# GpSimd instead of VectorE divides the attention probabilities by their sums

## The chip, the cores and the metric

The kernel runs on one core of a Trainium2 chip. The metric is the device time of one execution in microseconds (us); the core has a TensorE (PE), a VectorE (DVE), a ScalarE (ACT), a GpSimd (POOL) and a SyncE (SP), each with its own instruction queue, and they meet through semaphores that the kernel sets and waits for by hand.

## The reference, cut to what matters

Two layers of a trunk over 512 latent and 256 context tokens of width 1024, in float32. Both layers hold an attention with 8 heads; the rest (gated MLP, convolution module, ConvFFN, norms) stays as it is. In the first layer queries of latent tokens see all 768 keys, queries of context tokens the 256 context keys; in the second only the latent queries are needed. The part that matters is the softmax of `block_attention`:

```python
s = jnp.einsum('bqgrd,bkgd->bgrqk', q_blk, k, preferred_element_type=jnp.float32) * scale
p = jax.nn.softmax(s, axis=-1).astype(v.dtype)
return jnp.einsum('bgrqk,bkgd->bqgrd', p, v)
```

The division in it is done on the unnormalised probabilities exp(s - max): every row of 768 (or 256) values is multiplied by the reciprocal of its sum.

## The kernel before, in words

The whole network is one program. Each engine runs one long list of steps; the order of the steps is written out by hand, and counters (semaphores) say what may start. Both attentions use the same four functions: `attn_pe`, `attn_act`, `attn_dve` and, in the second alone, `attn_pool`. The first attention (semaphore family "eva") has 40 units, numbered from 0: units 0 to 31 are a head and a tile of 128 latent queries against 768 keys, units 32 to 39 a head and two tiles of context queries against 256 keys. The second (family "od") has 32 units, a head and a tile of 128 queries against 768 keys each.

A unit u goes this way. PE computes the scores (three matmuls for each bank in the first attention, five in the second, since float32 operands are split into a high and a low part). DVE takes the row maximum (L1624) and scales it (L1626). ACT takes the exponential and, in the same pass, the row sums `rsum` (L1594, with an accumulator read). DVE inverts the sums (L1632), drains its pipeline, and multiplies the probabilities in place by the inverse, one operand row at a time (`normalise`, L1635); its semaphore "p" lets PE transpose the probabilities (L1565). ACT copies the transposed ones to `PTe`/`PTo` (L1610), PE multiplies them with V (L1580), and DVE copies the result out (L1654).

The order on the queues: in its iteration u PE does transposes of u, scores of u+2, product with V of u, then what is put beside the unit. ACT does the exponential of u+1, the copy of the transposed u, the query copy of u+3 (L1503). DVE does `normalise(u+1)`, `maxima(u+2)`, in the first attention the low part of the query u+3, the copy out of u, then the work beside the unit. In the second attention that work is a part of the depthwise convolution of width 31: `conv_steps` (L2589, one tap on 128x512 values), three taps beside each of the units 2 to 13 and two beside the others, until all 124 are done. Beside the units stand also the pieces: projections of the second half of the keys and values on PE (units 0 to 5 for values, 7, 9, ..., 21 for keys, in turn 512 and 256 columns wide), with the subtraction of DVE for a key piece one unit later (L2697). POOL forms the low part of the queries in the second attention (`q_low` in `attn_pool`, L1662) and adds up channels near the end (L1886, L1889, L1896); in the first attention it gates the MLP half (L1864) and copies V (L1866), and is then idle until the output norm.

`Pe` has three buffers, `Pod` two, the sums `rsum` two.

Of the kernel before, what the change touches and what calls it, by code (L numbers as in the profile page):

```python
# [18 lines left out]
P = 128  # L19
F32 = mybir.dt.float32  # L20
F32R = mybir.dt.float32r
ALU = mybir.AluOpType
# [42 lines left out]
def build(nc, x, ctx, cvec, wpack, modw, modu, modb, normg, ffcw, rope_ev, rope_od, qkg, aln, wsT, bs,  # L65
          odcw, odcln, gcq, gckv, out):
    es = ExitStack()
    with es:
# [54 lines left out]
        rsum = const("rsum", [P, 2, 2])  # L123
# [485 lines left out]
        TURNED = (0, 2, 1, 3)  # L609
# [95 lines left out]
        def turned_place(g, t):  # L705

            return half_tokens(g, *((0, 0), (1, 1), (0, 1), (1, 0))[t])

        def turned_sum(dve, g, t):

            if t == 0:
                dve.wait_ge(S("pre3", "hi"), since("pre3", "hi") + KD * (g + 1))
                dve.wait_ge(S("pre3", "lo_even"), since("pre3", "lo_even") + KD // 2 * (g + 1))
            if t == 1:
                dve.wait_ge(S("pre3", "lo_odd"), since("pre3", "lo_odd") + KD // 2 * (g + 1))
            dve.drain()
            b11, b12, b21, b22 = (half_tokens(g, k, h) for k in range(2) for h in range(2))
            x, y = ((b12, b11), (b22, b11), (b22, b12), (b21, b22))[t]
            nc.vector.tensor_tensor(turned_place(g, t), x, y, ALU.subtract).then_inc(S("sv", f"tsum{g}"), 1)

        def turned_hi(act, g, t):

            act.wait_ge(S("sv", f"tsum{g}"), TURNED.index(t) + 1)
            if t == 3:
                act.wait_ge(w_used, F11 + 1)
            nc.scalar.activation(TH["ff1"][t][:, :, g, :], turned_place(g, t), ACT.Copy).then_inc(S("sv", "thi"), 1)
# [778 lines left out]
        def q_low(dve, u):  # L1505
# [3 lines left out]
            nc.vector.tensor_tensor(qTl[u % 2][:, 0:n], PS[:, 6, 0:n], qTh[u % 2][:, 0:n].bitcast(F32),  # L1509
                                    ALU.subtract).then_inc(S("eva", "qTl"), 1)  # L1510

        def attn_pe(pe, st, odd, U, lead=lambda: None, extra=lambda u: None):
            PT, Pb = (PTo, Pod) if odd else (PTe, Pe)

# [70 lines left out]
        def attn_act(act, st, odd, U, scale, extra=lambda u: None, values=lambda tiles: None):  # L1585
            PT, Pb = (PTo, Pod) if odd else (PTe, Pe)

            def exps(u):
                w, n = U[u][2], U[u][3] * P
                if u >= len(Pb):  # L1590
                    act.wait_ge(S(st, "ptr"), u - len(Pb) + 1)
                act.wait_ge(S(st, "max"), u + 1)
                for i in range(w):
                    last = nc.scalar.activation(Pb[u % len(Pb)][:, i * n:(i + 1) * n],  # L1594
                                                ps2(2 * (u % 2), w * n)[:, i * n:(i + 1) * n], ACT.Exp,
                                                bias=rmax[:, u % 2, i:i + 1], scale=scale,
                                                accum_out=rsum[:, u % 2, i:i + 1])
                last.then_inc(S(st, "exp"), 1)
# [16 lines left out]
        def attn_dve(dve, st, odd, U, scale, cat, extra):  # L1615
# [12 lines left out]
            def normalise(u):  # L1628
# [7 lines left out]
                                                   ALU.mult)  # L1636
                last.then_inc(S(st, "p"), 1)

            maxima(0)
            maxima(1)  # L1640
            if not odd:
                q_low(dve, 2)
            normalise(0)
            for u, (h, t, w, nk, k0) in enumerate(U):
                if u + 1 < len(U):
                    normalise(u + 1)
                if u + 2 < len(U):
                    maxima(u + 2)
                if u + 3 < len(U) and not odd:
# [7 lines left out]
        def attn_pool(pool, st, U, extra):  # L1657
# [5 lines left out]
                                        ALU.subtract).then_inc(S(st, "qTl"), 1)  # L1663
            for u in range(2):
                q_low(u)
            for u in range(len(U)):
                if u + 2 < len(U):
                    q_low(u + 2)
                extra(u)

        def rotate(dve, x0, x1, cs, sn, tA, tB):
# [154 lines left out]
        def _(pool):  # L1826
# [34 lines left out]
            for c in range(NT):  # L1861
# [2 lines left out]
                nc.gpsimd.tensor_tensor(cc, cc, Zv[:, c, :].rearrange("p (g q) -> p g q", q=P), ALU.mult)\  # L1864
                    .then_inc(S("gate", "gated"), 1)
            nc.gpsimd.tensor_copy(Vev[:, :, :], V32[:, :, :]).then_inc(S("gate", "vev"), 1)  # L1866
            out_then_norm_pool(pool, "evo", "pre1", NT)
            out_then_norm_pool(pool, "ffo0", "pre2", NT)
            power(pool, "odq", rstd[:, 0:LT])
# [982 lines left out]
```

## Time and the profile before

| | us |
|---|---|
| median of 3 runs (lowest to highest) | 1696.81 (1695.31 to 1699.03) |
| the profiled execution, its own time | 1694.81 |
| its span, first to last instruction | 1693.0 |
| PE, DVE, ACT, POOL busy in it | 1644.3, 1342.7, 824.9, 195.6 |
| mean granted TensorE clock | 0.996 |

The busy times come from the page of the profile. Durations of one instruction come from that one execution, whose own time is 1.8 us more than its span and 2.0 us less than the median. Line numbers (L...) are those of the kernel before. Where a row gives a time in brackets, that is how long the engine sat idle before the instruction, and who ended the wait.

### The profile page before, as it was taken

The numbers are of one execution on the slowest core, as the hardware profiler recorded it, in microseconds if no ns is written. First come the engines' busy times: TensorE is split into PE (matmuls) and PEld (weight loads), VectorE is DVE, ScalarE is ACT, GpSimd is POOL, SyncE is SP. The second block draws the span as 40 slices with busy tenths as digits, with TensorE's granted clock in tenths as the row PEclk, the third lists the DMA queues.
The fourth block names the chain that finished last, engine by engine and source line by source line (L and its number), as shares of the span: only waits on it lengthen the run. The fifth ranks groups of instructions, "written<-read, shape, count | busy, mean of one in ns | idle before, by whom it ended". The sixth has DMA issues, their size and how long they took to land.

```text
span 1693.0 us, 25933 instructions
## 1 busy us (share of the span) xinstructions
PE 1644.3 (97%) x9738; PEld 1478.7 (87%) x9738; DVE 1342.7 (79%) x2261; ACT 824.9 (49%) x1501; POOL 195.6 (12%) x201
## 2 busy tenths in 40 slices
PE   6999999999999999999999999999999999999998
PEld 4788899888999999998887888879888899999876
DVE  5676777767888999996888788978776799998554
ACT  4343256634435555554243534454455466666442
POOL 1078510000300000000000300011210200000000
PEclk9999999999999999999999999999999999999999
DMA  9633210051322444447563322200102223322331
GB/s 353 203 142 113 29 23 1 1 211 63 125 113 101 160 170 167 173 165 305 180 216 123 140 78 96 79 1 2 51 26 91 72 75 117 109 100 101 137 111 64
DMA packets 46059, 194.10 MB, mean 115 GB/s; under 512 B 13040, under 2 KB 13552, under 8 KB 31216
## 3 DMA queue, kind: packets, MB, share of 16 engines
q1 hardware_dynamic: 37248, 187.46, 31.1%
q10 hardware_dynamic: 8688, 4.99, 1.0%
q8 instruction: 78, 1.28, 0.3%
q14 instruction: 45, 0.37, 0.1%
HBM read 180.48 MB, written 11.96 MB: 114 GB/s over the span
## 4 chain that ended last, share of the span: by engine, by line
PE 44%; DVE 5%; ACT 2%; DVEq 1%; issue 1%; DMA 0%; ACTq 0%; POOL 0%
PE PS L1162 6%; PE PS L1168 6%; PE PS L1165 6%; PE PS L820 4%; PE PS L822 4%; PE PS L821 4%; PE PS L1580 2%; PE PS L326 2%; PE PS L334 2%; PE PS L330 2%; PE PS L1565 1%; DVE w_lo L315 1%; PE PS L362 1%; PE PS L358 1%; PE PS L361 1%
## 5 line engine op out<-in xcount | busy, mean ns | idle before, releaser
L1162 PE MATMUL PS<-w_hi,a_ring 128*128 128x512 f32 x670 | 262.8, 392 | 5.2 <-DVE A_ff_lo L1242 1.7
L1165 PE MATMUL PS<-w_lo,a_ring 128*128 128x512 f32 x670 | 260.8, 389 | 0.0
L315 DVE TENSOR_TENSOR w_lo<-w_raw,w_hi 128x2048 fp32r<-128x2048 f32 x62 | 143.9, 2321 | 105.8 <-ACT w_hi L309 100.6
L309 ACT ACTIVATE w_hi<-w_raw 128x2048 fp32r<-128x2048 f32 x62 | 118.6, 1914 | 163.1 <-PE PS L1162 104.0
L820 PE MATMUL PS<-TH_ff,FH_ff 128*128 128x256 f32 (+1 forms) x608 | 187.4, 308 | 2.8 <-ACT pu_ff L836 2.8
L822 PE MATMUL PS<-TH_ff,FL_ff 128*128 128x256 f32 (+1 forms) x608 | 187.3, 308 | 0.0
L821 PE MATMUL PS<-TL_ff,FH_ff 128*128 128x256 f32 (+1 forms) x608 | 187.2, 308 | 0.0
L1162 PEld LDWEIGHTS PS<-w_hi,a_ring 128*128 128x128 f32 x670 | 125.8, 188 | 34.9 <-DVE w_lo L315 2.6
L1165 PEld LDWEIGHTS PS<-w_lo,a_ring 128*128 128x128 f32 x670 | 125.8, 188 | 25.4
L820 PE MATMUL PS<-HT,FH_ff 128*128 128x256 f32 (+1 forms) x456 | 140.3, 308 | 0.0
L821 PE MATMUL PS<-HT,FH_ff 128*128 128x256 f32 (+1 forms) x456 | 140.3, 308 | 0.0
L822 PE MATMUL PS<-HT,FL_ff 128*128 128x256 f32 (+1 forms) x456 | 140.3, 308 | 0.0
L1391 POOL TENSOR_TENSOR rstd<-rstd,halfneg 128x1 f32<-128x1 f32 x20 | 11.0, 550 | 1094.7 <-DVE rstd L1337 1094.7
L1168 PE MATMUL PS<-w_hi,a_ring 128*128 128x512 f32 x334 | 130.0, 389 | 0.0
L820 PEld LDWEIGHTS PS<-TH_ff,FH_ff 128*128 128x128 f32 x608 | 115.9, 191 | 3.1 <-issue 3.0
L822 PEld LDWEIGHTS PS<-TH_ff,FL_ff 128*128 128x128 f32 x608 | 115.9, 191 | 0.0
L821 PEld LDWEIGHTS PS<-TL_ff,FH_ff 128*128 128x128 f32 x608 | 115.9, 191 | 0.0
L689 ACT ACTIVATE FH_ff<-Sw_ff 128x512 fp32r<-128x512 f32 x152 | 94.8, 626 | 32.2 <-PE PS L822 26.8
L698 DVE TENSOR_TENSOR FL_ff<-Sw_ff,FH_ff 128x512 fp32r<-128x512 f32 x152 | 103.9, 685 | 3.5 <-ACT FH_ff L689 1.6
L358 PE MATMUL PS<-w_hi,HT 128*128 128x512 f32 (+1 forms) x272 | 103.1, 379 | 0.4 <-DVE HT L2457 0.4
L326 PE MATMUL PS<-HT,w_hi 128*128 128x256 f32 (+1 forms) x352 | 103.3, 323 | 0.0
L361 PE MATMUL PS<-w_lo,HT 128*128 128x512 f32 (+1 forms) x272 | 102.1, 375 | 0.0
(369 smaller groups left out, 4196.0 us busy)
## 6 DMA issues: line engine op xcount, KB each, us to landing
w_raw<-wpack SPq DMA_DIRECT2D x102, 1024.0 KB, 4.9
m_raw<-modu SPq DMA_DIRECT2D x80, 512.0 KB, 5.8
mod_raw<-modw SPq DMA_DIRECT2D x8, 1024.0 KB, 11.6
a_kept<-yb SPq DMA_DIRECT2D x17, 384.0 KB, 2.3
c_rows<-c_scratch SPq DMA_DIRECT2D x8, 512.0 KB, 5.1
x_kept<-X SPq DMA_DIRECT2D x1, 3072.0 KB, 9.6
A_ff<-a_kept SPq DMA_DIRECT2D x2, 1536.0 KB, 8.4
X<-x_kept SPq DMA_DIRECT2D x1, 3072.0 KB, 10.1
```

What stands on the lines that cost most here:

```text
L309: nc.scalar.activation(w_hi[r][:, :], w_raw[r][:, :], ACT.Copy).then_inc(wh_ready, 1)
L315: nc.vector.tensor_tensor(w_lo[r][:, :], w_raw[r][:, :], w_hi[r][:, :].bitcast(F32), ALU.subtract).then_inc(wl_ready, 1)
L326: mm = nc.tensor.matmul(o, wh, xh, start=start, stop=False)
L358: mm = nc.tensor.matmul(o, xh, w_hi[r][:, wc], start=k == 0, stop=False)
L361: nc.tensor.matmul(o, xh, w_lo[r][:, wc], start=False, stop=False)
L698: nc.vector.tensor_tensor(FL[st][i][:, :, :], form_source(st, s, i), FH[st][i][:, :, :].bitcast(F32), ALU.subtract)\
L820: nc.tensor.matmul(o, wh, xh, start=begins, stop=False, skip_group_check=onto)
L821: nc.tensor.matmul(o, wh, xl, start=False, stop=False, skip_group_check=onto)
L822: last = nc.tensor.matmul(o, wl, xh, start=False, stop=ends, skip_group_check=onto)
L1162: mm = nc.tensor.matmul(o, ah, w_hi[n % 2][:, wc], start=k == 0, stop=False)
L1165: mm = nc.tensor.matmul(o, ah, w_lo[n % 2][:, wc], start=False, stop=False)
L1168: return nc.tensor.matmul(o, al, w_hi[n % 2][:, wc], start=False, stop=k == kt - 1)
```

## The change

DVE keeps the inversion of the sums, in a new function `invert` with a semaphore "rcp" of its own, shared by both attentions. The multiplication goes to POOL, in a new function `normalise_pool`: in the first attention for units 8 to 39 (units 0 to 7 stay with `normalise` on DVE, since `BY_VECTOR["eva"]` is 8), in the second for all 32. In the first attention POOL runs through them behind the copy of V; in the second unit u+1 is put behind the query part of u+2 in each iteration. ACT gets one more wait ahead of the exponential of u, for "p" of u-2, because its row sums go into the same buffer. Two semaphores of the second ConvFFN, `tsum0` and `tsum1`, become one, `tsum`, with its counts adapted; nothing is reordered there.

```diff
-            nc.vector.tensor_tensor(turned_place(g, t), x, y, ALU.subtract).then_inc(S("sv", f"tsum{g}"), 1)
+            nc.vector.tensor_tensor(turned_place(g, t), x, y, ALU.subtract).then_inc(S("sv", "tsum"), 1)
...
-            act.wait_ge(S("sv", f"tsum{g}"), TURNED.index(t) + 1)
+            act.wait_ge(S("sv", "tsum"), 2 * TURNED.index(t) + g + 1)
...
+        BY_VECTOR = {"eva": 8, "od": 0}
+
+        def rcp_count(st, u):
+
+            return u + 1 - BY_VECTOR[st] + (len(units(False)) - BY_VECTOR["eva"] if st == "od" else 0)
+
+        def normalise_pool(pool, st, U, u):
+
+            Pb = Pod if st == "od" else Pe
+            w, n = U[u][2], U[u][3] * P
+            pool.wait_ge(S("att", "rcp"), rcp_count(st, u))
+            if u:
+                pool.wait_ge(S(st, "p"), u)
+            for i in range(w):
+                pr = Pb[u % len(Pb)][:, i * n:(i + 1) * n]
+                last = nc.gpsimd.tensor_scalar(pr, pr, rsum[:, u % 2, i:i + 1], None, ALU.mult)
+            last.then_inc(S(st, "p"), 1)
...
                 act.wait_ge(S(st, "max"), u + 1)
+                if u >= 2:
+                    act.wait_ge(S(st, "p"), u - 1)
...
+            def invert(u):
+                dve.wait_ge(S(st, "exp"), u + 1)
+                sm = rsum[:, u % 2, 0:U[u][2]]
+                nc.vector.reciprocal(sm, sm).then_inc(S("att", "rcp"), 1)
...
-            normalise(0)
+            if BY_VECTOR[st]:
+                normalise(0)
+            else:
+                invert(0)
             for u, (h, t, w, nk, k0) in enumerate(U):
-                if u + 1 < len(U):
+                if u + 1 < BY_VECTOR[st]:
                     normalise(u + 1)
+                elif u + 1 < len(U):
+                    invert(u + 1)
...
             for u in range(2):
                 q_low(u)
+            normalise_pool(pool, st, U, 0)
             for u in range(len(U)):
                 if u + 2 < len(U):
                     q_low(u + 2)
+                if u + 1 < len(U):
+                    normalise_pool(pool, st, U, u + 1)
                 extra(u)
...
             nc.gpsimd.tensor_copy(Vev[:, :, :], V32[:, :, :]).then_inc(S("gate", "vev"), 1)
+            for u in range(BY_VECTOR["eva"], len(units(False))):
+                normalise_pool(pool, "eva", units(False), u)
             out_then_norm_pool(pool, "evo", "pre1", NT)
```

## Rows read from the trace of the kernel before

**Rows 1.** The page: busy time by engine, and the chain by engine.

```profile
PE 1644.3 (97%) x9738; PEld 1478.7 (87%) x9738; DVE 1342.7 (79%) x2261; ACT 824.9 (49%) x1501; POOL 195.6 (12%) x201
...
PE 44%; DVE 5%; ACT 2%; DVEq 1%; issue 1%; DMA 0%; ACTq 0%; POOL 0%
```

**Rows 2.** Busy time by stretch: start:end, length, PE, PEld, DVE, ACT, POOL, granted clock, DMA.

```profile
240.00:340.00 100.00, 97.02 (x722) 89.22 (x721) 73.90 (x197) 64.15 (x142) 0.00 (x0) 1.00 0.00 1
...
1162.00:1192.00 30.00, 29.54 (x211) 26.86 (x210) 28.09 (x57) 14.17 (x31) 4.42 (x6) 1.00 0.00 1
```

**Rows 3.** The transposes, second attention: all, then starts in the timeline (start, duration).

```profile
L1565 PE MATMUL PS<-ident,Pod x192: 269/272/328, 1117.0 to 1258.4; 128*128 128x128 f32 x192
...
1171.15 0.82 PE L1565 MATMUL PS<-ident,Pod 128*128 128x128 f32 x6
...
1176.79 0.27 PE L1565 MATMUL PS<-ident,Pod 128*128 128x128 f32 x1
...
1202.99 0.82 PE L1565 MATMUL PS<-ident,Pod 128*128 128x128 f32 x6
1206.73 0.82 PE L1565 MATMUL PS<-ident,Pod 128*128 128x128 f32 x6
1211.86 0.82 PE L1565 MATMUL PS<-ident,Pod 128*128 128x128 f32 x6
```

**Rows 4.** DVE's timeline in the second attention, one iteration.

```profile
1165.92 0.15 DVE L1632 RECIPROCAL rsum<-rsum 128x1 f32<-128x1 f32 x1
1166.15 0.62 DVE L1635 TENSOR_SCALAR Pod<-Pod,rsum 128x768 f32<-128x768 f32 x1
1166.69 0.95 DVE L1624 TENSOR_REDUCE rmax<-PS 128x1 f32<-128x768 f32 x1
...
1168.16 2.08 DVE L2589 SCALAR_TENSOR_TENSOR cat_od<-G,ccw,cat_od 128x512 f32<-128x512 f32 x3
1170.16 0.16 DVE L1632 RECIPROCAL rsum<-rsum 128x1 f32<-128x1 f32 x1
```

**Rows 5.** The timeline in the first attention, from a maximum to its transposes.

```profile
274.54 0.96 DVE L1624 TENSOR_REDUCE rmax<-PS 128x1 f32<-128x768 f32 x1
275.82 0.90 ACT L1594 ACTIVATE Pe<-PS,rmax 128x768 f32<-128x768 f32 x1 [0.90 <-DVE rmax L1626]
275.83 0.82 PE L1565 MATMUL PS<-ident,Pe 128*128 128x128 f32 x6
...
276.85 0.16 DVE L1632 RECIPROCAL rsum<-rsum 128x1 f32<-128x1 f32 x1 [0.53 <-ACT Pe L1594]
277.09 0.62 DVE L1635 TENSOR_SCALAR Pe<-Pe,rsum 128x768 f32<-128x768 f32 x1
...
279.02 0.27 PE L1565 MATMUL PS<-ident,Pe 128*128 128x128 f32 x1
...
336.10 1.13 PE L1580 MATMUL PS<-PTe,Vev 128*128 128x256 f32 x4 [1.57 <-ACT PTe L1610]
```

**Rows 6.** POOL's groups: operation, names, shapes, count; busy, mean ns; idle before.

```profile
L1873 POOL COPY QRD<-QR 128x1024 f32<-128x1024 f32 x4 | 4.2, 1042 | 27.1 <-DVEq L2652 27.1
...
L1866 POOL COPY Vev<-V 128x1536 f32<-128x1536 f32 x1 | 1.5, 1457 | 0.0
```

**Rows 7.** The timeline of POOL and DVE where both read SBUF.

```profile
1152.02 0.46 POOL L1662 TENSOR_TENSOR qNl<-QTn,qNh 128x128 fp32r<-128x128 f32 x1 [4.68 <-ACT qNh L1503]
...
1209.14 1.26 POOL L1886 TENSOR_TENSOR mu<-cat_od 128x512 f32<-128x512 f32 x1 [3.56 <-DVEq L2702]
...
1209.39 1.43 DVE L1635 TENSOR_SCALAR Pod<-Pod,rsum 128x768 f32<-128x768 f32 x1
```

**Rows 8.** The timeline at the last unit of the second attention.

```profile
1257.16 0.62 DVE L1635 TENSOR_SCALAR Pod<-Pod,rsum 128x768 f32<-128x768 f32 x1
...
1257.84 0.87 PE L1565 MATMUL PS<-ident,Pod 128*128 128x128 f32 x6 [0.21 <-DVE Pod L1635]
```

**Rows 9.** The timeline at the start of the second attention: a wait without a releasing engine.

```profile
1123.67 0.96 DVE L1624 TENSOR_REDUCE rmax<-PS 128x1 f32<-128x768 f32 x1 [5.08 <-remote]
```

## The prediction

> **What bounds the kernel now.** The page first: PE is busy 97% of the span and holds by far the largest share of the chain that ended last, DVE 5% of it [rows 1]. So a lighter DVE is worth only what DVE still holds in the two stages that change. The view by stretches says how much that can be: in 100 us of the first attention PE is busy 97.02, with DVE at 73.90; in the second attention there is a stretch of 30 us where DVE is busy 28.09 [rows 2]. That stretch, near 1162 to 1192, is the only one where DVE is close to full.
>
> Next the starts of PE's transposes, one set for each unit, since they show PE's own period. In the second attention an undisturbed unit without a piece takes 3.74 us (1202.99 to 1206.73) and one with a 512-wide piece 5.13 (1206.73 to 1211.86); the piece of 256 columns gives about 4.46 by the same reading. Unit 11 takes 5.64 where 5.13 would do (1171.15 to 1176.79) [rows 3]. Added up over all units, 31 periods from 1117.0 [rows 3] to 1257.84 [rows 8] (6 of 5.13 with pieces of the values, 4 of 5.13 and 4 of 4.46 with pieces of the keys, 16 plain ones of 3.75 and unit 30 of 2.0, and two sums over channels of 0.86), the matmuls alone would fill some 133 of 141 us. The 8 us between are: 2.3 at unit 1, 1.6 over units 10 to 15, 1.4 at units 21 and 22 (PE waits for its own last piece and for the subtraction behind it), 1.0 at units 25 and 27, 1.7 at unit 30 (no scores are left to fill the wait for the copy). In the first attention the period is 3.19 (275.83 to 279.02) [rows 5], and so for all latent units from 9 to 31 within 0.04; DVE and ACT wait there for PE and for one another, and PE is never out of work.
>
> **What the change removes.** 72 multiplications on DVE: 24 of 128x768 in the first attention, 16 of 128x256 there, 32 of 128x768 in the second. One of 768 takes 0.62, and from the inversion to the maximum behind it passes 0.77 (1165.92 to 1166.69), of which the inversion and its hand-over need about 0.15 [rows 4]. So DVE gets back 0.62 for each unit of 768. Where is that on the path? In the full stretch an iteration of DVE takes 4.24 with three taps (1165.92 to 1170.16) [rows 4], up to 4.64 with the subtraction of a key piece in it, against PE's mean of (3.74 + 5.13 + 3.74 + 4.46)/4 = 4.27. With 0.62 gone it is 3.6 to 4.0: PE sets the pace again, and the 1.6 us of units 10 to 15 come back. At unit 27 the exponential waits for DVE behind a large weight subtraction; 0.5 of that goes too, while unit 25 waits for ACT's own work and keeps its 0.5. That is 2.1 in all; I take 1.9. In the first attention the maxima already start as soon as the scores are there, so nothing is gained but at unit 38, where PE waits 1.57 for ACT's copy [rows 5], which stands behind the last exponential and that behind a maximum on DVE: an estimate of 0.5.
>
> **What it adds.** 72 multiplications on POOL, an operation that the trace does not show. The nearest rows are the copies, with one input of the same type: 1024 elements 1042 ns, 1536 elements 1457 ns, so 0.81 ns an element and 0.83 us for 768 [rows 6]. The other side is the operation with two inputs: 128 elements 0.46, 512 elements 1.26 [rows 7], 2.1 ns an element, 1.79 us for 768. I take 0.90, near the copy, because there is one tensor input and one scalar for each partition. Below 0.83 nothing speaks for it. The hand-over from DVE to POOL adds about 0.1, and as much again is in the wait for the semaphore by PE as before.
>
> Does the longer way, 1.15 instead of 0.85 from the start of the inversion to "p", reach PE? First attention: inversion at 276.85, product done at 277.71, transposes at 279.02, a slack of 1.31 [rows 5]. The maximum comes about 0.1 earlier too. Counting from there, a product of up to 1.9 us on POOL is hidden, and for the context units two of 256 columns are hidden up to about 1.5 together (by the copy's line they take 0.84, by two inputs 1.45). Second attention: the taps stand ahead of the inversion on DVE, so the slack is least behind three taps and a subtraction, with the short piece next (units 10 and 14). There the inversion comes 2.95 after the transposes of the unit before, "p" 0.3 + d later for a product of d, and PE wants it at 4.46: hidden up to d = 1.2. By the same count, in the round of four units with three taps the other three hide up to 1.8, 2.1 and 2.5, and units without taps more. So at 0.90 nothing inside is late. Only the last unit shows: PE waits there for the product on DVE, 1257.16 to 1257.78, and starts at 1257.84 [rows 8]; POOL's makes that 0.3 later, with nothing left to cover it.
>
> The wait on POOL's queue: in the second attention the query part of u+3 (0.46 [rows 7]) is queued behind the product of u+1. It was done over 2 us before its scores, and still is by 1 us. Unit 0's product stands ahead of the query part of unit 2; the product is done near 1115.6, the query part at 1116.1, and the scores come at 1117.6. ACT's added wait, for the product two units back, is met long before: PE's transposes of that unit, which ACT or PE already wait on, need it too. The merged semaphore costs nothing, DVE issues the eight sums in just the order of the new counts; were it otherwise, up to one 0.7 us sum. In the first attention POOL had nothing to do from unit 8 to the output norm, so nothing is queued behind its waits. No DMA moves, and SP's queue waits on none of it.
>
> Sum: 1694.8 - 1.9 - 0.5 + 0.3 = 1692.7 for an execution like the profiled one; that one stands 2.0 under the median, so 1694.7 as a median.
>
> **The shared way into SBUF.** Of one DVE product the trace says more: at 1209.39 it took 1.43 instead of 0.62, ending 0.42 after a POOL addition that had begun at 1209.14 and took 1.26 [rows 7]. The two did not overlap. The Trainium skill (SBUF — State Buffer, Who interferes with whom) has it that such a DVE operation, or one with two SBUF inputs, and a POOL operation exclude each other for their whole length; by that rule, which this row agrees with, the taps would wait for POOL's products. Here is where it would act: a tap starts 2.24 after the start of the inversion (1165.92 to 1168.16) [rows 4], 1.6 once the product is gone. POOL's product runs from 0.25 to 1.15 after it, beside the maximum, which reads PSUM. With d = 0.90 there is no overlap; above 1.35 there is, at 12 units with three taps. For the speed of the product itself, the GPSIMD Engine Reference of the Trainium skill (Performance versus the Vector engine) gives 1.03 to 1.8 cycles an element for short one-input loops, which would be 0.66 to 1.15 us plus the dispatch; the sum by its middle would be the same to 0.1, and no row here shows it.
>
> **Rivals.**
> 1. *The product on POOL goes at the rate of two inputs*, 1.79. For: the scalar operand is an input that the copies lack. Against: it is one value for a partition. Then taps wait 0.45 at 12 units, "p" is 0.6 late at units 10 and 14, and the last unit loses 1.2: of 2.4 gained 1.2 are lost again inside and 1.2 at the end (beside the 0.3 of the forecast counted in it), the net is nothing: 1696.8.
> 2. *POOL becomes the late hand in every unit* (slower). From d = 1.9 each unit of the first attention is late by half of what d exceeds it, since the loop from scores to transposes spans two units, and in the second attention the units with taps go first. At d = 2.0 that is 24 x 0.05 = 1.2, in the three rounds of four units with taps 3 x (0.8 + 0.2) = 3.0, and 1.4 at the last unit, against 2.4 gained: 1700. At 2.4 it is 24 x 0.25 = 6.0, 3 x (1.2 + 0.6 + 0.3) = 6.3 and 1.8: 1708.5. It decides from 2.0 on. For: POOL's durations stretch when DVE reads SBUF. Against: both rates in the trace lie under the point.
> 3. *Fetching the instructions moves.* At unit 1 DVE's maximum waits 5.08 for nothing that an engine did [rows 9]; it goes on at once after a single transfer on the instruction queue at 1123.3, and PE loses 2.3. The streams of DVE and POOL change in length. If this wait goes, 1692.4; if one like it comes up at another place, 1697 to 1699.
> 4. *The freed time buys nothing*, all of it being hidden: 1696.8 or 0.3 more. Against: DVE's 28.09 of 30 us.
>
> **How the numbers follow.** Forecast 0.55, rival 1 0.10, rival 2 0.09, rival 3 0.12 for the better way and 0.07 for the worse, rival 4 0.07. The most that the stages have left, 8 us, caps the gain. A measurement of this kernel can tell about 0.2%, 3.4 us, so "faster" means below 1693.4 and "slower" above 1700.2. Faster: rival 3's better way at 0.11 and a lucky 0.1 of the forecast, 0.21. Slower: rival 2 with 0.08, rival 3 with 0.03, 0.02 from the others, 0.13. Within: 0.66. The range takes in rival 3 downwards and the near end of rival 2 upwards: 1691 to 1700.5.
>
> **What would show it.** In the profile after: POOL's products at 0.8 to 1.0 us (above 1.35 rival 1, above 1.9 rival 2); DVE's product gone from all but units 0 to 7; a period of 5.13 at unit 11 instead of 5.64; taps still at 2.1 to 2.2 for three; the first attention's period still 3.19; the last transposes waiting for POOL instead of DVE, 0.3 later behind the inversion. The forecast is wrong if PE's transposes wait for POOL anywhere before the last unit, or if the weight of the difference lies outside the two attentions.

## The result, and the profile after

| | before | after |
|---|---|---|
| median, us (lowest to highest, runs) | 1696.06 (1693.90 to 1699.03, 4) | 1713.41 (1711.66 to 1719.64, 4) |
| span of the profiled execution | 1693.0 | 1717.9 |

The change makes the kernel slower by 17 us: the ratio is 1.0107, with a 95% interval of 1.0087 to 1.0127. That is 18.7 over the forecast of 1694.7 and 12.9 over the end of its range. The profiled execution of after is the longest of its four (1719.64; the spans of the other three are 1709.9 to 1711.7). Its second attention has 5.3 us more than that of the run with four buffers of sums (below), from a longer wait at its start and a lower clock behind waits; so where a size matters, that run stands in for it.

The page of after, busy time and chain:

```profile
PE 1653.5 (96%) x9738; PEld 1481.2 (86%) x9738; DVE 1306.5 (76%) x2189; ACT 828.1 (48%) x1501; POOL 329.4 (19%) x273
...
PE 43%; DVE 5%; ACT 2%; issue 1%; POOL 1%; DVEq 1%; POOLq 0%; another core or an unknown queue 0%; DMA 0%; ACTq 0%
```

VectorE has its 72 multiplications and 36 us less than in [rows 1], as meant. GpSimd has 134 us more, where the forecast's prices, 56 times 0.90 and 8 times 0.84, would have been some 57. The groups by line say why:

```profile
L1527 POOL TENSOR_SCALAR Pod<-Pod,rsum 128x768 f32<-128x768 f32 x32 | 70.6, 2206 | 67.0 <-DVE rsum L1662 60.2 <-issue 6.8
L1527 POOL TENSOR_SCALAR Pe<-Pe,rsum 128x768 f32<-128x768 f32 x24 | 52.9, 2205 | 47.0 <-DVE rsum L1662 47.0
...
L1527 POOL TENSOR_SCALAR Pe<-Pe,rsum 128x256 f32<-128x256 f32 x16 | 14.6, 923 | 8.6 <-DVE rsum L1662 8.6
```

Each group line gives the count, the busy time and the mean of one in ns. A product of 768 columns takes 2.20 us on GpSimd. The forecast took 0.90, between 0.83 from the copies [rows 6] and 1.79 from the two-input operations [rows 7]: the value lies outside both ends. The line through 768 and 256 columns is 0.28 us and 2.5 ns an element.

Who waited for line L1527, from the view of one source line:

```profile
who waited for it (us, times):
  PEld PS L1583: 19.2, 29
  PE PS L1583: 11.4, 25
```

PE's transposes (L1583 now) wait for GpSimd 25 times, which the prediction had named as the sign that it is wrong. The first attention, in the place of [rows 5] (start, duration, and in brackets the idle time before and who ended it):

```profile
276.50 0.87 PE L1583 MATMUL PS<-ident,Pe 128*128 128x128 f32 x6 [0.19 <-POOL Pe L1527]
...
277.16 0.16 DVE L1662 RECIPROCAL rsum<-rsum 128x1 f32<-128x1 f32 x1 [0.51 <-ACT Pe L1614]
...
277.42 2.20 POOL L1527 TENSOR_SCALAR Pe<-Pe,rsum 128x768 f32<-128x768 f32 x1 [0.97 <-DVE rsum L1662]
...
279.72 0.83 PE L1583 MATMUL PS<-ident,Pe 128*128 128x128 f32 x6
```

The product ends at 279.62 and the transposes start at 279.72: the slack that was 1.31 beyond the old product is used up. From the start of one unit's transposes to those of the next (the period of the unit) it is now 3.22 and 3.55 in turn, a mean of 3.39 instead of 3.19. The second attention, from unit 9 to unit 10, in the place of [rows 3] and [rows 4]:

```profile
1175.46 0.82 PE L1583 MATMUL PS<-ident,Pod 128*128 128x128 f32 x6
1176.55 2.07 DVE L2624 SCALAR_TENSOR_TENSOR cat_od<-G,ccw,cat_od 128x512 f32<-128x512 f32 x3
1178.54 0.15 DVE L1662 RECIPROCAL rsum<-rsum 128x1 f32<-128x1 f32 x1
...
1178.79 2.20 POOL L1527 TENSOR_SCALAR Pod<-Pod,rsum 128x768 f32<-128x768 f32 x1 [3.23 <-DVE rsum L1662]
1180.07 2.28 DVE L2624 SCALAR_TENSOR_TENSOR cat_od<-G,ccw,cat_od 128x512 f32<-128x512 f32 x3
...
1181.05 0.88 PE L1583 MATMUL PS<-ident,Pod 128*128 128x128 f32 x6 [0.97 <-POOL Pod L1527]
```

The inversion comes 3.08 after the transposes before it (the prediction counted 2.95), the product ends 2.45 later, and the period is 5.59 instead of 4.47: 1.1 late. And later, at units 27 and 28, GpSimd's queue:

```profile
1260.33 1.26 POOL L1931 TENSOR_TENSOR sqs<-sqs,sqs 128x512 f32<-128x512 f32 x1 [0.16 <-issue]
1261.55 0.46 POOL L1692 TENSOR_TENSOR qNl<-QTn,qNh 128x128 fp32r<-128x128 f32 x1
1261.98 2.21 POOL L1527 TENSOR_SCALAR Pod<-Pod,rsum 128x768 f32<-128x768 f32 x1
1264.35 1.28 POOL L1931 TENSOR_TENSOR sqs<-sqs,sqs 128x512 f32<-128x512 f32 x1 [0.17 <-issue]
```

The sum over channels (L1931), the query part (L1692) and the product (L1527) follow one another without a gap, 4.02 from one sum to the next, more than PE's period of 3.75. In the same stretch PE waits for the query part:

```profile
1262.06 0.50 PE L1556 MATMUL PS<-KNh,qNh 128*128 128x512 f32 x1 [0.96 <-POOL qNl L1692]
```

The last unit, in the place of [rows 8]:

```profile
1279.53 2.20 POOL L1527 TENSOR_SCALAR Pod<-Pod,rsum 128x768 f32<-128x768 f32 x1 [5.21 <-DVE rsum L1662]
1281.79 0.88 PE L1583 MATMUL PS<-ident,Pod 128*128 128x128 f32 x6 [1.55 <-POOL Pod L1527]
```

And the wait without a releasing engine at the start of the second attention, which was 5.08 in [rows 9], with the granted clock by stretch behind it (start:end, length, PE, PEld, DVE, ACT, POOL, clock, DMA):

```profile
1131.20 0.96 DVE L1644 TENSOR_REDUCE rmax<-PS 128x1 f32<-128x768 f32 x1 [6.45 <-remote]
1131.95 2.29 PE L1598 MATMUL PS<-PTo,Vod 128*128 128x128 f32 x9 [5.47 <-ACT PTo L1630]
```

```profile
1130.00:1140.00 10.00, 8.05 (x41) 7.31 (x42) 3.37 (x7) 5.19 (x8) 3.09 (x3) 0.68 0.01 2
1140.00:1150.00 10.00, 10.00 (x68) 8.90 (x67) 8.46 (x15) 4.98 (x10) 3.77 (x3) 1.00 0.00 0
```

PE had waited 5.47; in the 10 us in which it goes on, the granted clock has a mean of 0.68, between its two levels of 1.2 and 2.4 GHz, and then it is full again.

### The profile page after: what moved, and what is told of

Its sections match the earlier page's. It is cut to its first block, busy times and chain, and to the rows that moved or that the text cites. A ratio compares the mean times of both kernels' runs of the same rounds, so it can differ in the third digit from the quotient of the medians.

```text
span 1717.9 us, 25933 instructions
## 1 busy us (share of the span) xinstructions
PE 1653.5 (96%) x9738; PEld 1481.2 (86%) x9738; DVE 1306.5 (76%) x2189; ACT 828.1 (48%) x1501; POOL 329.4 (19%) x273
## 4 chain that ended last, share of the span: by engine, by line
PE 43%; DVE 5%; ACT 2%; issue 1%; POOL 1%; DVEq 1%; POOLq 0%; another core or an unknown queue 0%; DMA 0%; ACTq 0%
PE PS L1162 6%; PE PS L1168 6%; PE PS L1165 6%; PE PS L820 4%; PE PS L821 4%; PE PS L822 4%; PE PS L1598 2%; PE PS L326 1%; PE PS L334 1%; PE PS L330 1%; POOL Pod L1527 1%; DVE w_lo L315 1%; ACT w_hi L309 1%; PE PS L1583 1%; PE PS L361 1%
## 5 line engine op out<-in xcount | busy, mean ns | idle before, releaser
L1644 DVE TENSOR_REDUCE rmax<-PS 128x1 f32<-128x768 f32 (+1 forms) x72 | 66.7, 926 | 74.6 <-PE PS L1560 40.6
```

## The experiments

All are compared with the kernel before on the same chip. The table sums the periods of the transposes, read from the timeline of one profiled execution each, over parts of the two attentions. It says where the time went; the ratios say how much of it is clear of noise.

| profiled execution of | 1st: units 8 to 31 | 31 to 39 | 2nd: units 0 to 2 | 2 to 8 | 8 to 20 | 20 to 31 |
|---|---|---|---|---|---|---|
| before | 73.73 | 22.89 | 12.58 | 29.43 | 52.89 | 45.98 |
| after | 78.11 | 23.14 | 18.19 | 29.44 | 55.43 | 54.88 |
| a, first attention alone | 78.08 | 23.13 | 11.40 | 29.44 | 52.50 | 45.97 |
| b, second alone | 73.76 | 22.87 | 14.01 | 29.45 | 55.34 | 53.55 |
| d, four buffers of sums | 78.26 | 23.17 | 14.22 | 29.44 | 55.44 | 53.56 |
| c, copy | 73.70 | 20.51 | 11.05 | 29.45 | 51.26 | 47.43 |
| g, copy twice | 73.66 | 22.91 | 13.01 | 30.59 | 53.67 | 52.48 |
| h, constant | 77.22 | 22.94 | 12.88 | 30.55 | 55.03 | 52.66 |
| e, short query part | 78.16 | 23.14 | 12.31 | 30.30 | 54.52 | 53.77 |
| f, short sums | 78.16 | 23.12 | 12.47 | 30.54 | 55.41 | 51.04 |
| j, both queue works short | 78.16 | 23.13 | 11.44 | 30.28 | 54.54 | 50.33 |
| i, split | 73.34 | 21.32 | 12.22 | 29.43 | 52.16 | 48.63 |
| k, maximum first | 73.72 | 24.71 | 14.06 | 29.44 | 52.87 | 45.96 |
| l, half of the context units | 73.34 | 21.33 | 10.95 | 29.44 | 52.87 | 45.97 |

The column of units 0 to 2 holds the wait without a releaser. It differs from run to run and follows no edit in a way that I could name. The last column also holds some clock: in the rows after, g and e the granted clock has a mean of 0.73 to 0.75 over unit 27, just behind a wait of PE, and in d it is 1.00 there. For the same order of work that unit takes 6.60 in after and 5.03 in d.

**One attention alone.** Two runs split the change. In the first GpSimd has the products of the first attention only, in the second those of the second only.

```diff
-        BY_VECTOR = {"eva": 8, "od": 0}
+        BY_VECTOR = {"eva": 8, "od": 32}      # a; b: {"eva": 40, "od": 0}
```

> The multiplication goes to GpSimd in the first attention alone (units 8 to 39); the second is as before. Theory 1, the product on GpSimd takes 2.2 us and is late in every unit of 768 keys: the first attention keeps its 4.6 us (periods of 3.22 and 3.55 in turn instead of 3.19), 1700.5 in all, and nothing else moves. Theory 2, the loss is made by GpSimd's queue in the second attention (query parts and channel sums between the products): 1696 to 1697. Theory 3, the added wait of ScalarE: like theory 1 in the time, but with ScalarE's exponentials late.

> The multiplication goes to GpSimd in the second attention alone; the first is as before. Theory 1: some 12 us of the 17 are here, 1708 to 1709, so that the costs of the two attentions add up to the whole. Theory 2: the whole, 1712 to 1713. If the sum of this and the first-attention-only kernel is clearly under or over 17 us, something outside the two stages plays a part.

In each run the added wait of ScalarE, and in a GpSimd's calls, are left out of the other attention too. The first alone is 1702.26 us (nine of ten runs from 1698.67 to 1705.63, the tenth 3319.88, which nothing here explains; ratio 1.0033, 1.0019 to 1.0046), the second alone 1706.56 (1.0054, 1.0037 to 1.0071). Both lose, and together they give 0.0087 of the 0.0107: the rest lies within the intervals. In the table each attention has in its own run the periods of d, and in the other run those of before, to 0.4 us outside units 0 to 2. So the two losses are separate, and nothing outside the attentions is needed. (1700.5 and 1708 to 1709 were expected.)

**A copy in the place of the product.** The probabilities stay undivided, so that only the time of a GpSimd operation of 0.83 us is tried.

```diff
-                last = nc.gpsimd.tensor_scalar(pr, pr, rsum[:, u % 2, i:i + 1], None, ALU.mult)
+                last = nc.gpsimd.tensor_copy(pr, pr)
```

> The changed kernel with a copy of the probabilities onto themselves on GpSimd in place of the multiplication: every wait, queue and semaphore as in the change, but the division by the sum is left out. By the copies of the kernel before it should take 0.83 us where the product takes 2.2. Theory 1, the duration is the whole cost: the forecast comes true, 1694 to 1696, no transposes waiting for GpSimd before the last unit. Theory 2, the queue's order costs by itself: 1700 to 1706. Theory 3, ScalarE's added wait: above 1705, as the wait is still there.

1692.74 us, ratio 0.9979 (0.9968 to 0.9989). Waits, queues and semaphores are those of the change, and only the length differs:

```profile
L1527 POOL COPY Pod<-Pod 128x768 f32<-128x768 f32 x32 | 26.4, 825 | 95.4 <-DVE rsum L1662 87.2 <-issue 8.2
```

So the length of the product alone turns a gain of 3.6 us (0.0021) into a loss of 17. Theory 1 holds. The relief that the prediction counted at units 10 to 15 is there: units 8 to 20 take 51.26 instead of 52.89, 1.63 for a forecast of 1.6. Two things were not forecast. The context units (31 to 39) win 2.4 us. And units 20 to 31 lose 1.45, of which 0.19 is the last unit's and 1.20 that of unit 27, where PE waits not for the product but for the query part:

```profile
1235.55 0.82 POOL L1527 COPY Pod<-Pod 128x768 f32<-128x768 f32 x1 [3.52 <-DVE rsum L1662]
1236.54 1.27 POOL L1931 TENSOR_TENSOR sqs<-sqs,sqs 128x512 f32<-128x512 f32 x1 [0.16 <-issue]
1237.76 0.90 POOL L1692 TENSOR_TENSOR qNl<-QTn,qNh 128x128 fp32r<-128x128 f32 x1
...
1238.72 0.50 PE L1556 MATMUL PS<-KNh,qNh 128*128 128x512 f32 x1 [1.41 <-POOL qNl L1692]
```

GpSimd stood 3.52 waiting for the inversion, then came the copy and the sum over channels, and only then the query part, though ScalarE had its input ready at 1234.59. In the kernel before, the query part stood ahead of that sum. So the order on GpSimd's queue costs 1.2 at this unit even at a length of 0.83; theory 2 has a small share in the copy run.

**The added wait of ACT.** With four buffers for the sums ACT needs no wait for "p".

```diff
-        rsum = const("rsum", [P, 2, 2])
+        rsum = const("rsum", [P, 4, 2])
...
-                if u >= 2:
-                    act.wait_ge(S(st, "p"), u - 1)
```

> The changed kernel with four buffers for the row sums instead of two, so that the exponential needs no wait for the product two units back, and the wait is taken out. Theories 1 and 2: no difference to the changed kernel, 1712 to 1714. Theory 3, the added wait holds ScalarE back: most of the 17 us come back, below 1702.

1713.61 us, 1.0102 (1.0085 to 1.0119), against the 1.0107 of the change: the wait costs nothing that can be told, and theory 3 falls. The table agrees: in the first attention and in units 2 to 20 both have the same times to 0.15.

**What is queued on GpSimd.** In one run only the first column of the query's low part is formed (the others are zero), in one only the first column of the last five of the six channel sums beside the units, in one both.

```diff
-                nc.gpsimd.tensor_tensor(qNl[u % 2][:, :], QTn[:, h, t * P:(t + 1) * P], qNh[u % 2][:, :].bitcast(F32),
+                nc.gpsimd.tensor_tensor(qNl[u % 2][:, 0:1], QTn[:, h, t * P:t * P + 1], qNh[u % 2][:, 0:1].bitcast(F32),
...
-                    add = nc.gpsimd.tensor_tensor(sqs[0][:, :], sqs[0][:, :], sqs[j][:, :], ALU.add)
+                    add = nc.gpsimd.tensor_tensor(sqs[0][:, 0:1], sqs[0][:, 0:1], sqs[j][:, 0:1], ALU.add)
```

> The changed kernel; in the second attention GpSimd forms only 1 of 128 columns of the query's low part (the others are zero), with the same waits and signals, so about 0.3 us less for each unit on its queue. Theory 1, the product's own length is the whole loss: 1712 to 1713.5, as the change. Theory 2, the query part queued behind the product holds up the scores: 3 to 5 us come back, 1708 to 1710, and PE's scores wait for GpSimd no more (5.1 us in 10 waits in the profile of the change).  Mixed: 1710 to 1712.

> The changed kernel; of GpSimd's six sums over channels near the end of the second attention (1.26 us each) the last five add 1 of 512 columns only, with the same waits and signals. They stand between the products on its queue at units 19 to 21 and 26 to 28, just where the changed kernel's periods are longest (up to 6.1 us instead of 4.6). Theory 2: 2 to 4 us come back, 1709 to 1711.5. Theory 1: no more than 0.5.

> The changed kernel with both of GpSimd's other works in the second attention cut to one column: the low part of the queries (left out but for one column, so PE multiplies zeros) and the sums over channels beside units 12 to 31 (left out but for one column). If both only lengthen GpSimd's queue, each at its own units, their gains add: e_short_query gave 1.9 and f_short_sums 3.2 under the changed kernel's 1713.4, so some 1708 to 1709, and 11 to 12 over the kernel before stay, which are the product's own length. Rival: the queue is what matters, and with all of it gone the time falls to within 5 of the kernel before, 1701 or less.

1711.53 us (1.0085, 1.0064 to 1.0106), 1710.23 (1.0085, 1.0063 to 1.0108), and 1706.41 for both (1.0067, 1.0044 to 1.0090). The first is what e called mixed, the second theory 2 of f, the third lies under the 1708 to 1709 of j. By the ratios each takes 0.0022 off the change's 0.0107 and both take 0.0040, each figure uncertain by some 0.002: they add as far as can be told. With the queue nearly empty some 11 us stay (7 to 15 by the interval), which rules out the rival of j, 1701 or less. So the queue is the smaller part: some 7 us by the ratios, 4.1 by the periods of units 8 to 31 (104.87 in j, 109.00 in d, 98.87 before). One of the waits that remain in j, at unit 25:

```profile
1238.78 1.29 DVE L2747 TENSOR_TENSOR cat_od<-cat_od,mu 128x512 f32<-128x512 f32 x2
1239.99 0.16 DVE L1662 RECIPROCAL rsum<-rsum 128x1 f32<-128x1 f32 x1
...
1240.24 2.20 POOL L1527 TENSOR_SCALAR Pod<-Pod,rsum 128x768 f32<-128x768 f32 x1 [4.24 <-DVE rsum L1662]
...
1242.50 0.87 PE L1583 MATMUL PS<-ident,Pod 128*128 128x128 f32 x6 [0.98 <-POOL Pod L1527]
```

No taps stand here, but VectorE's other work beside the unit (L2747) does, and holds the inversion just as they did.

**A length between the two.** Two copies behind each other, 0.83 each with a drain between, end 1.79 after the first starts. That brings the forecast's upper bound of 1.79 to a trial (the division is left out again).

```diff
+                nc.gpsimd.tensor_copy(pr, pr)
+                pool.drain()
+                last = nc.gpsimd.tensor_copy(pr, pr)
```

> The copy kernel with the copy done twice, a drain of GpSimd's pipeline between: some 1.75 us instead of 0.83 or 2.2; the division by the sum is left out. By the slack counted in the prediction (1.9 us in the first attention's latent units, 1.2 to 2.5 in the second): the latent units of the first attention stay at 3.19, the second attention loses 2 to 4 us at units with taps or sums and at the last; 1695.5 to 1698.5. If the loss grows evenly with the length instead (1692.7 at 0.83, 1713.4 at 2.2), 1706.

1703.61 us (1.0040, 1.0027 to 1.0054). Neither expectation was met: it is 5 over the 1698.5 that the prediction's slack gave, and 2 under an even growth with the length. The latent units of the first attention keep their 3.19 (73.66 for units 8 to 31), so the slack of 1.9 that the prediction gave them is not passed. But the second attention loses 6.5 us in units 20 to 31 already at this length (of it some 1.6 by the lower clock at unit 27, an estimate from 6.60 less 5.03 above). This also answers rival 1: at its own price of 1.79 it counted 1696.8, no gain and no loss, and the run loses 7.

**Is it the operand?** The scalar for each partition is replaced by the constant 1.0, with nothing else changed (the division is left out).

```diff
-                last = nc.gpsimd.tensor_scalar(pr, pr, rsum[:, u % 2, i:i + 1], None, ALU.mult)
+                last = nc.gpsimd.tensor_scalar(pr, pr, 1.0, None, ALU.mult)
```

> The changed kernel with the constant 1.0 in place of the sum's inverse: the same operation on GpSimd without an operand read for each partition; the division is left out. If the operand is what makes it 2.2 us instead of the copy's 0.83, it takes 0.8 to 1.2 and the kernel 1692.5 to 1695. If the operation itself does, it takes 2.2 and the kernel 1713.

1709.90 us (1.0075, 1.0054 to 1.0096), some 5 less than the change by the ratios, each uncertain by some 3.5, and 3 less than the expected 1713; the operation is hardly shorter:

```profile
L1527 POOL TENSOR_SCALAR Pod<-Pod 128x768 f32<-128x768 f32 x32 | 68.2, 2132 | 66.2 <-DVE rsum L1662 65.5 <-issue 0.7
```

The operation as such is the slow one, 2.13 against 0.83 for the copy; reading the scalar adds 0.07. That it multiplies isn't the reason: in the kernel before, six products of two tensors of 128x512 on GpSimd (L1864) take 1.25 to 1.76 each, the shortest no longer than a sum of that size. What in this operation takes the time no run shows.

**The product split.** GpSimd multiplies columns 512 to 767 (of a context unit the second block), VectorE the rest behind its inversion.

```diff
-            for i in range(w):
-                pr = Pb[u % len(Pb)][:, i * n:(i + 1) * n]
+            for i in range(w)[-1:]:
+                pr = Pb[u % len(Pb)][:, 512:768] if w == 1 else Pb[u % len(Pb)][:, i * n:(i + 1) * n]
...
                 nc.vector.reciprocal(sm, sm).then_inc(S("att", "rcp"), 1)
+                dve.drain()
+                pr = Pb[u % len(Pb)][:, 0:512 if U[u][2] == 1 else 256]
+                nc.vector.tensor_scalar(pr, pr, sm[:, 0:1], None, ALU.mult).then_inc(S("sv", "tsum"), 1)
```

PE and ScalarE also wait for VectorE's part, through a counter of its own.

> The changed kernel, but GpSimd multiplies only columns 512 to 767 of the 768 (of a context unit only its second block of 256), and VectorE the rest itself, behind the inversion and a drain. GpSimd's part should take 0.92 us by the channels run with 256 columns, VectorE's part of 512 some 0.42. Theory A (the length of GpSimd's operation is all that costs): the probabilities are ready 1.1 to 1.3 after the inversion starts, under the slack of 1.2 plus hand-over at every unit with taps, so the periods come back to those of the kernel before but for the last unit (+0.3): 1695 to 1698. Rival B (the two operations can't use SBUF together): VectorE's part is held to the end of GpSimd's and lasts 0.9 to 1.3 instead of 0.42, the maximum behind it is late by as much, VectorE carries 0.3 to 0.6 more a unit than in the kernel before, and the units with three taps lose it: 1700 to 1705, with the first attention's period at 3.2 to 3.3.

1694.94 us, ratio 0.9993 (0.9981 to 1.0005): no difference from before. The timeline, one unit:

```profile
276.78 1.19 POOL L1527 TENSOR_SCALAR Pe<-Pe,rsum 128x256 f32<-128x256 f32 x1 [1.98 <-DVE rsum L1666]
276.78 0.49 DVE L1669 TENSOR_SCALAR Pe<-Pe,rsum 128x512 f32<-128x512 f32 x1
```

Theory A holds in the time, with a correction: VectorE's part was not held to the end of GpSimd's, as rival B had it, but GpSimd's took 1.19 where 256 columns alone took 0.92. Here it is GpSimd's that is longer. And the periods don't all come back: units 20 to 31 lose 2.65, most of it at unit 27 (5.48 for 4.24, where PE waits 1.42 for the query part as in the copy run) and the last (4.30 for 3.71), and the context units win 1.57 in return.

**The loop in the context units.** The copy run had won 2.4 us there. I took it for a loop in which exponential, product, maximum and the next exponential wait for one another, and put the maximum first, in the kernel before.

```diff
+                late = not odd and u + 1 >= 8 * LT and u + 2 < len(U)
+                if late:
+                    maxima(u + 2)
                 if u + 1 < len(U):
                     normalise(u + 1)
-                if u + 2 < len(U):
+                if u + 2 < len(U) and not late:
                     maxima(u + 2)
```

> The kernel before, with one thing changed on VectorE: in the context units of the first attention (from u+1 = 32 on) the maxima of u+2 stand ahead of the product of u+1. Nothing goes to GpSimd. Theory: the 2.85 us period of these units is set by a loop, exponential, product, maximum, exponential, and not by a load; the copy on GpSimd gained 2.4 us there only since the product left this loop. Then the period falls to 2.3 to 2.6 here too, and the time to 1693.5 to 1695.5. Rival: VectorE's load gained the 2.4; then the order changes nothing, 1696 to 1697, and the product being later makes PE's transposes wait for it.

1697.26 us, 1.0009 (0.9996 to 1.0021). The period is 3.16, not 2.3 to 2.6 but longer than 2.85. Half of the theory fell, and the wait that the rival foresaw, PE's transposes waiting for the later product, is there. Its other half, VectorE's load, does not fit: in the kernel before VectorE stood idle for 0.49 in each of these units, waiting for the exponential (at 321.05, 323.90, 326.75). The timeline of k:

```profile
324.65 0.16 DVE L1632 RECIPROCAL rsum<-rsum 128x2 f32<-128x2 f32 x1
...
324.88 0.62 DVE L1635 TENSOR_SCALAR Pe<-Pe,rsum 128x256 f32<-128x256 f32 x2
...
325.55 0.66 PE L1565 MATMUL PS<-ident,Pe 128*128 128x128 f32 x4 [0.68 <-DVE Pe L1635]
...
326.96 0.69 DVE L1624 TENSOR_REDUCE rmax<-PS 128x2 f32<-128x512 f32 x1 [0.80 <-PE PS L1547]
```

The product, now behind the maximum, makes the transposes late, the scores stand behind the transposes on PE, and the next maximum waits for the scores. Product and maximum are in a loop whichever stands first; of the edits tried, those that gave some of the product to another engine shortened it.

**A version that beats both.** The split, in the eight context units alone; everywhere else the products are those of the kernel before, and GpSimd's calls and ScalarE's added wait are taken out of the second attention.

```diff
-        BY_VECTOR = {"eva": 8, "od": 0}
+        BY_VECTOR = {"eva": 32, "od": 32}     # and the split above
```

> A version meant to be kept: only in the eight context units of the first attention (32 to 39) does GpSimd multiply one of the two blocks of 256 columns, VectorE the other; everywhere else VectorE multiplies as in the kernel before. In the split run these units had a period of 2.60 instead of 2.85, and the second attention as a whole gained nothing. Theory: the product is in a loop of VectorE's and ScalarE's alone, and only taking a part of it off VectorE, not a new order, shortens it; the second attention is then that of the kernel before. Gain 1.9 us from the starts of units 31 to 39: 1694 to 1696, ratio 0.9985 to 0.9995, which is at the edge of what can be told. Rival: the gain of these units is given back by a later start of what follows or is lost in the wait for instructions at the start of the second attention: 1696 to 1698, while the period of 2.60 still shows.

1691.64 us (1690.82 to 1692.79) beside 1695.96 for the kernel before: ratio 0.9970 (0.9958 to 0.9982): by the ratios faster than both kernels, and below the 1694 to 1696 that was expected. The context units have the period of 2.60:

```profile
324.94 0.35 DVE L1669 TENSOR_SCALAR Pe<-Pe,rsum 128x256 f32<-128x256 f32 x1
324.94 1.06 POOL L1527 TENSOR_SCALAR Pe<-Pe,rsum 128x256 f32<-128x256 f32 x1 [1.53 <-DVE rsum L1666]
...
326.16 0.60 PE L1585 MATMUL PS<-ident,Pe 128*128 128x128 f32 x4
```

They give 1.56 us (22.89 to 21.33), the rest of both attentions is that of before to 0.4, and the start of the second is 1.63 shorter in this execution. The median's gain of 4.3 is more than the 1.56 that the edit explains; whether the shorter start comes from the edit stays open.

## Why the prediction was wrong, step by step

**The step that failed** is the price of the product under "What it adds": "Below 0.83 nothing speaks for it", 1.79 above, and 0.90 taken "because there is one tensor input and one scalar for each partition". It measured 2.20. Both bounds were rows of other operations, and the number of inputs was taken as what sets GpSimd's speed. The constant instead of the scalar (2.13, with one tensor input like the copy's 0.83) shows that it is not. The copy in the same place gives 1692.74 for the forecast's 1694.7. That the two lie so near is partly luck: a gain of 2.4 in the context units and a loss of 1.2 at unit 27 are in it, and neither was forecast. Rival 2 had the mechanism, GpSimd as the late hand "from 2.0 on", with 0.09 of the chance.

**The second failed step** is the slack in the second attention: three of four units with taps were to hide 1.8 to 2.5, "and units without taps more". By rival 2's own formula 2.20 gives 24 x 0.15 = 3.6 in the first attention, 4.5 at the taps and 1.6 at the end against 2.4 won, 1704.1. Measured is 1713.4. In the table the tap units fit: 8 to 20 take 55.44 with four buffers, 2.55 over before; 4.5 less the relief of 1.6 would be 2.9. What the formula lacks are units 20 to 31: 7.58 over before, of which only 1.6 was counted, the last unit's. There are two causes. The first is the slack. The trace of before already had the row; the prediction read the large weight subtraction at unit 27 for what it could win there, not for what it leaves ahead of the transposes:

```profile
1238.21 2.42 DVE L2691 TENSOR_TENSOR w_lo<-w_raw_in_lo,w_hi 128x2048 fp32r<-128x2048 f32 x1
...
1240.55 0.15 DVE L1632 RECIPROCAL rsum<-rsum 128x1 f32<-128x1 f32 x1
1240.78 0.62 DVE L1635 TENSOR_SCALAR Pod<-Pod,rsum 128x768 f32<-128x768 f32 x1
...
1241.54 0.82 PE L1565 MATMUL PS<-ident,Pod 128*128 128x128 f32 x6
```

The inversion comes 0.99 before the transposes. With 0.25 for the hand-over that hides a product of 0.74, not of 2.5. The other lengths agree: the copy ends at 1236.37 and its transposes start at 1236.47 without a wait, so 0.83 is just hidden; at 1.79 they wait 0.76 and at 2.20 1.21, with periods ahead of them of 4.66 and 5.12 for 3.74. The second is the queue. "Still is by 1 us" counted the query part behind the product, but not behind the sums over channels as well; at unit 27 this costs already at 0.83 (above), and in d PE also waits 0.98 for a channel sum itself. Without both queue works 4.35 of the 7.58 stay, so the queue holds 3.2 there.

This step would have failed the forecast at a price inside its bounds too. Summed over the columns of the table but that of units 0 to 2, the copy (0.83) wins 2.6 us on before, two copies (1.79) lose 8.4 and the product (2.20, in d) loses 15.0; in the 8.4 is the low clock of unit 27. A straight line between the first two passes zero near 1.1 us, an estimate from these sums; the prediction put the loss beyond 1.8.

**The rest.** Rival 2's sum at 2.20, divided by place, beside what the run with four buffers shows over the kernel before:

| us over before | by rival 2's formula | measured |
|---|---|---|
| first attention, units 8 to 39 | 3.6 - 0.5 = 3.1 | 4.8 |
| second, units 0 to 8 | 0 | 1.65 |
| units 8 to 20 | 4.5 - 1.6 = 2.9 | 2.55 |
| units 20 to 31 | 1.6 - 0.3 = 1.3 | 7.6 |
| sum | 7.3 | 16.6 |

In the first attention 0.20 is lost for each period where 0.15 was counted: 2.13 and 2.20 both put the turning point near 1.8, not 1.9. Of the 0.5 at unit 38 0.35 came (its period is 2.78 for 3.13), and units 31 to 37 lost more than that. In units 0 to 8 it is the wait of [rows 9] in another size; no edit of these runs governs it, and it is 11.05 in the copy run and 14.22 here for the same order of work, so I leave it open. Rival 3 set this wait down to the fetching of instructions, since a transfer on the instruction queue started at 1123.23 and VectorE went on at 1123.67. The other traces don't bear that out: in c the transfer starts at 1122.71, 2.5 after VectorE went on (1120.23), in d 1.0 after, and in the profile after at 1134.45, 3.3 after. The span's whole difference is 17.7; the last 1.1 lie outside these stretches.

**What held.** The removal and the relief (1.63 for 1.6). The slack of 1.9 in the first attention, to 0.1: 3.19 at two copies, 3.39 at 2.20. The slack of 1.2 at the unit with three taps and a subtraction: 1.0 late by it, 1.1 measured. ACT's added wait at nothing; the merged semaphore was in the copy run too, which gained. The last unit: at 0.83 its period is 0.2 longer (3.90 for 3.71), at 2.20 1.6 (5.31). **What was missed on the other side** is the gain in the context units. The prediction costed them by their slack and found that "nothing is gained but at unit 38", although VectorE sat idle for 0.49 before each of their inversions and PE could run them in 2.3 to 2.6 (the copy run). That is 2.4 us, more than the 1.9 counted for the second attention.

## What to carry to other kernels

An operation that no row shows has no bounds from other operations of the engine. Leave its price open in the range, and work out first from which length the result turns. Slack is the least distance from the producer to the consumer over all units, to be read in the timeline at each kind of work that stands ahead of the producer, not derived from the kind that one had in mind. An operation put at the head of an in-order queue also holds back everything queued behind it while it waits: count all of that, not only the next in line. Where a loop of hand-overs through two engines set the period, a new order on one of them did not shorten it here; half of the work on an idle engine did.

## What was not expected of the hardware

GpSimd multiplies 128x768 float32 values by a scalar in 2.20 us and by a constant in 2.13, and copies them in 0.83. For 256 columns they are 0.92, 0.85 and 0.40. So this operation on one tensor (2.5 ns an element) is dearer here than a sum of two tensors, which took 1.26 for 512 columns [rows 7], or a product of two (1.25, L1864 before), where this line gives 1.56. The forecast had cited the GPSIMD Engine Reference of the Trainium skill (Performance versus the Vector engine) for 1.03 to 1.8 cycles an element. The estimate of 0.66 to 1.15 us from it is not what these runs show for this operation (2.20), and the measurement decides.

GpSimd's product and VectorE's product did not run fully side by side. GpSimd's 256 columns took 0.92 alone, 1.06 beside a VectorE product of 0.35 and 1.19 beside one of 0.49: started together, it ended 0.71 and 0.70 after VectorE's. With the taps, which read two tensors, it was different. In the run with four buffers:

```profile
1164.68 2.21 POOL L1527 TENSOR_SCALAR Pod<-Pod,rsum 128x768 f32<-128x768 f32 x1 [2.49 <-DVE rsum L1660]
...
1166.03 2.27 DVE L2622 SCALAR_TENSOR_TENSOR cat_od<-G,ccw,cat_od 128x512 f32<-128x512 f32 x3
1166.86 0.89 POOL L1690 TENSOR_TENSOR qNl<-QTn,qNh 128x128 fp32r<-128x128 f32 x1
```

The taps start in the middle of the product. The first lies beside the product and takes 0.743, the second beside the product's end and takes 0.744, as taps with GpSimd idle do (mean 0.746). The same holds for all 12 taps of that attention that lie beside a product for over 0.1 us: 0.743 to 0.753, and the products stay at 2.20 to 2.21. GpSimd's operation with two tensor inputs is another matter: it takes 0.89 here for 0.46, the third tap, which lies beside it alone, 0.787, and the eight taps like that one have a mean of 0.88.

The rule of the Trainium skill that the prediction weighed (SBUF — State Buffer, Who interferes with whom) was read there as naming two kinds of VectorE operation that exclude a GpSimd operation for their whole length. For the multiplication by a scalar the split runs agree as far as they go: it is as if all but the first 0.2 us of GpSimd's product came after VectorE's had ended (an estimate, 0.92 less 0.71). For an operation with two SBUF inputs beside a GpSimd operation that reads SBUF, the taps beside the product don't agree: by the rule they would have waited until 1166.89, and here the measurement decides.
